# The down weights of experts four to sixteen move from SyncE's DMA queue to ScalarE's

## The reference

```python
def _grouped_moe(x, w_router, b_router, w_gu, w_down):
    ...                       # softmax router, best group of 4, top 2 experts in it
    for e in range(N_EXPERTS):                    # 16
        g, u = jnp.split(t @ w_gu[e], 2, axis=-1) # 1024 x 1024
        y = (jax.nn.silu(g) * u) @ w_down[e]      # 512 x 1024
        out = out + gate[:, e:e + 1].astype(y.dtype) * y
    return out.reshape(B, S, D)
```

## Time and profile before

| | before |
|---|---|
| median of three runs | 672.95 us |
| the profiled execution's own time | 673.94 us |
| its span (first to last instruction) | 672.2 us |
| PE busy | 645.9 us (96%) |
| DVE busy | 290.9 us (43%) |
| ACT busy | 146.7 us (22%) |
| HBM read | 229.87 MB |
| granted TensorE clock | 0.997 of full speed |

### The profile page before, as it was taken

The page is one execution under the profiler, slowest core; times in us unless marked ns, Lnnn a source line. Parts: engine busy times, 40 slices in busy tenths (PEclk is TensorE's granted clock), DMA queues, the critical chain, the costliest instruction groups (busy, mean ns, idle before and its releaser), DMA issues.

```text
span 672.2 us, 7170 instructions
## 1 busy us (share of the span) xinstructions
PE 645.9 (96%) x2750; PEld 287.0 (43%) x2750; DVE 290.9 (43%) x770; ACT 146.7 (22%) x331; POOL 22.6 (3%) x41
## 2 busy tenths in 40 slices
PE   6999999999999999999989998999999999999983
PEld 5854564564333333333324455456333333343321
DVE  0010303477354353443564254468444535336356
ACT  1030342231121211211231051333112021021212
POOL 2030100000000000000000011200000000000000
PEclk9999999999999999999999999999999999999998
DMA  9999917175999999999999971846899999999991
GB/s 306 386 405 355 424 75 257 57 256 195 399 423 420 422 421 422 421 419 422 422 418 411 421 298 41 338 144 239 324 424 421 422 421 420 421 421 421 421 374 65
DMA packets 41447, 231.43 MB, mean 344 GB/s; under 512 B 10169, under 2 KB 10169, under 8 KB 15810
## 3 DMA queue, kind: packets, MB, share of 16 engines
q1 hardware_dynamic: 36976, 230.72, 84.8%
q10 hardware_dynamic: 4434, 0.21, 0.5%
HBM read 229.87 MB, written 1.05 MB: 344 GB/s over the span
## 4 chain that ended last, share of the span: by engine, by line
PE 84%; DMA 9%; DVE 4%; SPq 1%; POOL 1%; issue 1%; ACT 1%; POOLq 0%; DVEq 0%
PE pb L679 29%; PE pb L478 19%; PE pb L709 14%; DMA ring<-in_w_down 8%; PE pb L537 4%; PE pb L729 3%; PE pb L851 2%; PE pb L652 2%; PE pb L631 1%; PE pb L428 1%; PE pb L654 1%; PE pb L446 1%; DMA ring<-in_w_in_a 1%; PE pb L435 1%; PE pb L595 1%; POOL bufA L409 1%
## 5 line engine op out<-in xcount | busy, mean ns | idle before, releaser
L478 PE MATMUL pb<-ring,hT 128*128 128x512 f32 x320 | 143.8, 597 | 0.8 <-DVE hT L1688 0.8
L709 PE MATMUL pb<-ring,bufC 128*64 128x512 f32 x512 | 117.4, 597 | 3.3 <-DMA ring<-in_w_down 3.3
L679 PE MATMUL pb<-ring,hT 128*64 128x512 f32 x512 | 113.7, 593 | 0.4 <-DMA ring<-in_w_gu 0.4
L679 PE MATMUL pb<-ring,bufB 128*64 128x512 f32 x480 | 106.4, 593 | 0.0
L1474 DVE STREAM_TRANSPOSE bufC<-bufC 32x128 f32<-32x128 f32 x256 | 103.1, 403 | 3.8
L1500 DVE COPY bufA<-pb 32x512 f32<-32x512 f32 x64 | 43.7, 683 | 121.8 <-PE pb L709 120.8
L478 PEld LDWEIGHTS pb<-ring,hT 128*128 128x128 f32 x320 | 58.6, 190 | 65.8 <-issue 63.7
L679 PEld LDWEIGHTS pb<-ring,hT 128*64 128x64 f32 x512 | 36.3, 137 | 72.1 <-issue 70.0
L709 PEld LDWEIGHTS pb<-ring,bufC 128*64 128x64 f32 x512 | 34.6, 136 | 72.0 <-issue 65.2
L1077 ACT ACTIVATE bufA<-pb 32x512 f32<-32x512 f32 x64 | 37.7, 589 | 114.8 <-PE pb L709 114.0
L679 PEld LDWEIGHTS pb<-ring,bufB 128*64 128x64 f32 x480 | 33.9, 137 | 67.2 <-issue 65.4
(11 more groups left out here) (245 smaller groups left out, 434.0 us busy)
## 6 DMA issues: line engine op xcount, KB each, us to landing
ring<-in_w_gu SPq DMA_DIRECT2D x124, 1024.0 KB, 21.8
ring<-in_w_down SPq DMA_DIRECT2D x64, 1024.0 KB, 23.7
ring<-in_w_in_a SPq DMA_DIRECT2D x11, 1024.0 KB, 19.0
ring<-in_w_out_a SPq DMA_DIRECT2D x4, 1024.0 KB, 20.9
ring<-in_w_q_b SPq DMA_DIRECT2D x4, 1024.0 KB, 23.3
ring<-in_w_out_b SPq DMA_DIRECT2D x4, 1024.0 KB, 23.7
bufA<-in_w_gu SPq DMA_DIRECT2D x2, 1024.0 KB, 6.2
hT<-in_w_gu SPq DMA_DIRECT2D x2, 1024.0 KB, 8.5
```

The lines of the kernel that those rows point to most:

```text
L478: last = mm(pb[bank][:, :], hT[:, k, t * P:(t + 1) * P], slot(i0 + k // 2)[0][:, k % 2, c * HALF:(c + 1) * HALF], start=k == 0, stop=k == ...
L679: last = mm(pb[0][c * 64:(c + 1) * 64, :].rearrange("p (a n) -> p a n", a=2), xe[m % 2][:, k, g * SLOTS:(g + 1) * SLOTS], w.rearrange("p ( ...
L709: last = mm(to[c * 64:(c + 1) * 64, :], heT[u == EXPERTS - 1][:, (2 * hf + j) * 64:(2 * hf + j + 1) * 64], w[:, j, c * HALF:(c + 1) * HALF ...
```

## The change

Thirteen of the sixteen experts' down weights in each layer, those of experts 3 to 15, are no longer issued by SP. ACT issues them on its own queue. It issues those of expert u + 3 behind `silu(u + 2)` or, for every fourth expert, behind `take_y` of the expert three before. The buffers, the place numbers, the semaphores and the wait on `freed` stay the same. SP keeps all gate/up weights, the down weights of experts 0 to 2, and all other weights, in the old order.

```diff
@@ in SP's program, layer 0 (and the same in layer 1)
                 if u == 2:
                     load_side(0, 0)
-                load_down(u_dn(0, u), w_down[0, ORDER[u]])
+                if u < 3:
+                    load_down(u_dn(0, u), w_down[0, ORDER[u]])
@@ in ACT's program, inside moe(l)
+                def load_down(u):
+
+                    v = w_down[l, ORDER[u]].rearrange("(p q j) n -> p q j n", q=2, j=2)
+                    for q in range(2):
+                        buf, got = slot(u_dn(l, u) + q)
+                        act.wait_ge(freed, u_dn(l, u) + q - RING + 1)
+                        act.dma_start(buf[:, :, :], v[:, q]).then_inc(got, 16)
+
...
                     take_y(u)
                     silu(u + 2)
+                    load_down(u + 3)
                     if more:
                         take_x(m + 1, 0)
                         take_x(m + 1, 1, 3)
...
                     take_y(u + 1)
                     silu(u + 3)
                     if more:
+                        load_down(u + 4)
+                    if more:
                         take_x(m + 1, 2)
                         take_x(m + 1, 3, 3)
                     take_y(u + 2)
                     if more:
                         silu(u + 4)
+                        load_down(u + 5)
                     take_y(u + 3)
+                    if more:
+                        load_down(u + 6)
```

More of the change, by code:

```diff
@@ L349, in _ @@
                     load_side(1, 0)
-                load_down(u_dn(1, u), w_down[1, ORDER[u]])
+                if u < 3:
+                    load_down(u_dn(1, u), w_down[1, ORDER[u]])
             spill(1)
```

## The result

The changed kernel takes **697.0 us** (median of four runs, 693.6 to 702.0) against 673.5 us before (also four runs now; the 672.95 above was the median of three). The ratio is 1.034, 95% interval 1.025 to 1.042, so it is slower by 17 to 28 us. The forecast was 696 us, range 683 to 712.

The account below looks back on a forecast made before the run. It took PE and the DMA engines, arriving together at each layer's end, to bound the kernel. Per layer 3.8 us of added idle time plus 7.6 at the end, 22.8 for both, on 672.95 gave 696 us, range 683 to 712.

Parts of the forecast that it names:

- What bounds the kernel: In the experts, PE and DMA engines arrive together; DMA idle time after about 166 us moves the layer's end as much.
- SP's saved issues: SP loses 26 issues per layer, but nobody waits for SP itself in the late stretch: 0.
- ACT's added issues: 26 per layer on ACT, about 0.9 us a pair, hidden behind PE's work: 0, at most 6 us in all.
- The gap: At each layer's start of experts, expert 3's down weights go out later and DMA engines idle longer: 3.8 us per layer.
- The tail: At each layer's end a gate/up piece lands last, leaving PE 9.6 us of work, not 1.96: 7.6 us more.
- the sign that this step is wrong: A down piece landing last in a layer would show the 7.6 us for the order of last landings wrong.
- The total: 11.4 us per layer, 22.8 for both, taking the median from 672.95 to 696 us, +3.4%.
- half of the tail's cost absent: Lower end of the forecast's own range, given as 686 us: half of the 7.6 us per layer not occurring.
- Equal shares: In the experts, two queues with full pieces each get half of the DMA engines' rate.
- Rival B: ACT's queue gets a third of the engines or less, 34 us per layer, 740 us or more; chance 0.08.
- rival C: Two queues move more bytes between 182 and 345 us; no longer slower from 453 GB/s, 670 us at best; chance 0.04.
- Rival A, by which only the sequencers change: Landing order and total stay; only 3.8 us idle per layer is left, 681 us, or 673 without it; chance 0.10.

Follow-up runs that it names:

- e5: Kernel before, one queue: SP issues expert 3's down weights behind the gate/up weights of expert 5, in both layers; 680.0 us, ratio 1.009.
- e3: Changed kernel, but SP again issues the down weights of experts 3, 14 and 15 in their old places, ACT those of 4 to 13; 684.6 us, ratio 1.015.
- e7: Kernel before, SP issuing all weights, plus 52 ACT DMAs of 512 B at the changed kernel's places and behind the same waits; 678.1 us, ratio 1.006.
- e4: Kernel before, one queue: SP issues the down weights of experts 14 and 15 ahead of the gate/up weights of 15; 689.3 us, ratio 1.023.
- e1: Changed kernel, but SP again issues the down weights of experts 14 and 15 in their old place, ACT those of 3 to 13; 685.8 us, ratio 1.017.
- e2: Changed kernel, but SP again issues expert 3's down weights in their old place, ACT those of 4 to 15; 689.8 us, ratio 1.025.
- e10: Changed kernel, but ACT issues only the down weights of experts 6 to 13, each behind silu(u) of its own expert, SP all others; 676.2 us, ratio 1.003.
- e6: Changed kernel, but ACT issues each pair of down weights one expert earlier, behind silu(u + 1) for expert u + 3; 697.8 us, ratio 1.034.

## Why the prediction was right

*What bounds the kernel.* Right. e5 moved the end by a gap of DMA time, e3 by waits of PE. Neither had slack.

*SP's saved issues, 0.* Right: the rate stayed at 421 GB/s.

*ACT's added issues, 0.* Right: 0.33 to 0.98 us each, 0.40 in the median, and PE never waits for ACT in the changed kernel's experts. e7 bounds it from above at 3.8 us, and its lower rate accounts for about as much.

*The gap, 3.8 us per layer.* Right in place and nearly in size; e5 measured 2.9 for its 3.4 us part. In the changed kernel the experts of layer 0 begin 0.9 us earlier in the profiled run (158.11 became 157.23 for the gate/up piece issued there). The 66th of the 70 pieces lands at 339.07 there and at 335.04 before, so the DMA engines are 4.0 + 0.9 = 4.9 us behind; in layer 1, reckoned the same way, 4.0.

*The tail, 7.6 us per layer.* Right for what PE waits for last, and in size by e4 (15.7 us for 15.2). Its 9.6 us of work behind that landing measured 9.9 in layer 1 and 11.1 in layer 0; the additional 1.5 us are TensorE's clock (below). Two things in it were wrong. First, a gate/up piece doesn't land last: a down(15) piece does, at 350.0 against 348.1, which the prediction had named as the sign that this step is wrong. The step holds all the same, since PE needs that piece only at 355.5. Second, it read two rows one expert too high. The row at 294.21 is take_y(10) and the one at 311.90 is silu(13); take_y(11) and silu(14) come at 305.03 and 326.42. So the pairs of 14 and 15 couldn't go out at 295.5 and 312.3. In the changed kernel they went out at 311.3 and 336.1, the second that late because PE was behind. They were still in time, so the sum didn't suffer.

*The total.* From the first matmul of expert 0 to the end of down(15) a layer takes 13.0 us longer in layer 0 and 11.0 in layer 1, where 11.4 was forecast for each; with the 0.9 us of the earlier start that is the 23.2 us of the profiled executions. That the median comes within 1 us is partly luck: the gap was longer than 3.8, the slow clock was not in the sum, and the last awaited piece was the 69th to land and not the 70th. (One slip in the range: half of the tail's cost absent would be 688, not 686.)

*Equal shares.* Right, 4.96 us between the landings of a pair. Rival B is out with it, and rival C with the 421 GB/s.

*Rival A, by which only the sequencers change.* Out. This kernel lost 3.4%: the two queues keep separate orders, and the order and the later start were worth that much. The Trainium skill's page "DMA: Bandwidth & Descriptors", section "Issuing engines are not separate DMA queues", says that issuing from several engines saves only time on the sequencer. The trace agrees for the rate, 421 GB/s with one queue and with two; the time changed all the same.

*What was incomplete.* The prediction treats the loss as gap plus tail, as if taking both away would give all back, and each alone its own part. e3 shows that 11 us remain, and the traces of e1 and e2 that either one alone leaves the same. Two chains run side by side. The DMA chain (gap 3.8, tail 7.6) gives 11.4 us per layer. The PE chain (waits in gate_up(11) to gate_up(13), with slower matmuls after them) gives 5.2 to 6.5 us per layer in e1, e2 and e3 and is hidden beneath the first, because PE would wait for the last piece of gate_up(15) anyway. The total was right because the longer chain was; removing a part of the longer one uncovers the shorter. The loss in the middle is a term that the prediction didn't have.

## What to carry to other kernels

When the DMA engines are full, two queues with pieces of 1 MB shared them half and half here, so moving a third of the bytes to a second queue lands that third early and the rest late; keep in one queue what has to land in the order of use, or issue on the second one just in time (e10). Look at the last piece of each stretch, because what the compute engine still has to do behind its landing is added to the time in full. When two chains end together, make one run without all the suspected causes at once, since it shows a loss that they hid (e3), and read the trace even of a run whose time is the expected one (e2).

## What the runs showed of the hardware

I had not counted on PE's clock. In the kernel before it is 1.00 through the experts. In the changed one, stretches of 2 us after the waits of layer 0, and at last a stretch and a group of matmuls of layer 1:

```profile
302.00:304.00 2.00, 0.00 (x0) 0.00 (x0) 0.00 (x0) 0.00 (x0) 0.00 (x0) 1.00 1.01 418
304.00:306.00 2.00, 1.79 (x6) 0.68 (x8) 0.00 (x0) 0.00 (x0) 0.00 (x0) 0.66 1.01 422
306.00:308.00 2.00, 2.00 (x6) 0.49 (x4) 0.06 (x1) 0.38 (x1) 0.00 (x0) 0.50 1.02 426
308.00:310.00 2.00, 2.00 (x12) 0.72 (x10) 0.36 (x1) 0.00 (x0) 0.00 (x0) 0.98 1.01 422
...
350.00:352.00 2.00, 2.00 (x8) 0.62 (x6) 0.54 (x2) 0.38 (x1) 0.00 (x0) 0.50 1.03 414
...
671.00:680.00 9.00, 7.93 (x36) 2.61 (x38) 5.42 (x12) 1.56 (x3) 0.00 (x0) 1.00 0.03 8
...
671.59 1.94 PE L681 MATMUL pb<-ring,hT 128*64 128x512 f32 x8 [2.74 <-DMA ring<-in_w_gu]
```

In layer 0, after waits of 1.6 and 2.4 us close together, and again after one of 2.8, the granted clock is 0.50, the 1.2 GHz level, and then returns to 2.4. Eight matmuls took 3.28 us in place of 1.94. So a DMA wait of PE can cost more than its own length: in e3, 4.6 us of waits brought 2.9 us of slower matmuls. This is also most of the 5.6 us by which PE is busier on the page: in layer 0 the slow groups (3.28, 4.01, 2.83 and 4.45 us for 1.94, 3.6, 1.94 and 3.6) make 3.5 us, and layer 1 has one such dip, at 628 to 632 us.

It doesn't follow every such wait. In layer 1 the wait of 2.74 us before the last piece of gate_up(15) left the clock at 1.00, and the eight matmuls took 1.94 us. In layer 1 of e6, waits of 1.65 and 2.41 us close together and a later one of 3.02 left it at 1.00, while one of 2.22 us brought 0.50. No dip came after the waits of the kernel before (0.3 to 0.6 us in the experts) nor after those of 1.57 and 0.70 us in the changed one. The traces give no rule by the length of a wait.

Also unexpected: with 52 DMAs of 512 bytes in packets of 4 bytes beside the weights the rate was 416 GB/s in place of 421, and the kernel took 3.8 us longer (e7, interval 2.4 to 5.2). Tiny packets were not free while the engines were full.
